# Products of a zeroed tile in front of TensorE's waits in a four-layer encoder step

## The chip, the cores and the metric

The kernel runs on one core of a Trainium2 chip. The metric is the device time of one execution in microseconds (us). The engines are TensorE (PE; its weight loads are shown apart as PEld), VectorE (DVE), ScalarE (ACT), GpSimd (POOL) and SyncE (SP), which issues most DMAs. Each engine works through its own instructions in the order of the program, and they meet at semaphores: `wait_ge` holds an engine until a count is reached, `then_inc` raises it when an instruction ends.

## The reference

One inference step of a trunk of four layers on 320 rows of width 1024 (64 rows of a running stream, 256 of a new one). Each layer is RMSNorm, a token mixer, a residual add, RMSNorm, a gated feed-forward block with a causal convolution of width 3, and a residual add. The mixers are, in order: sparse attention with an indexer (layer 0), an RWKV-7 state mixer (layer 1), multi-head latent attention (layer 2), sparse attention again (layer 3).

```python
hn = _rmsnorm(x, w['n_mix'][i])
# layers 0, 3: q, k, v, qi, ki, wi = split(h @ w_in); top keys by the indexer; softmax; @ w_out
# layer 1:
xx = h_prev - h
xm = h[:, :, None, :] + xx[:, :, None, :] * mu
r, k, v = xr @ w_rkv[0], xk @ w_rkv[1], xv @ w_rkv[2]
w_log = -softplus(-(w0 + tanh(xw @ w1) @ w2)) - 0.5
a = sigmoid(a0 + (xa @ a1) @ a2);  g = sigmoid(xg @ g1) @ g2
kk = normalise(k * k_k);  k = k * (1 + (a - 1) * k_a)
y, S = _wkv7_scan(S0, r, decay, k, v, -kk, kk * a)
y = groupnorm(y) + sum(r * k * r_k) * v
out = (y * g) @ w_out
x = x + out
x = x + (silu(gate) * val) @ w_down      # gate, val: convolution of rmsnorm(x) @ w_up
```

The outputs are the rows of y, the new keys, values and latents, and the states.

## The kernel before, in words

Activations lie transposed: 128 partitions of the width, 320 rows in the free dimension, eight such tiles for the width 1024. All dense weights stream through two slots as numbered slabs: SP loads a slab into `raw`, ACT copies it to `hi` (rounded to fp32r, L1749), DVE or POOL subtracts to `lo` (L2294, L681). `product` (L960 to L972) multiplies a slab's 128 columns with an activation tile in three fp32r products per contraction step: hi by XH (L968), hi by XL (L969), lo by XH (L970). Small products are plain fp32 calls.

There is no scheduler: the order of the work is the order in which each engine's program is written, and `ready(n)` or a `wait_ge` marks what TensorE needs next. The places that matter here, all in TensorE's program:

- `dsa` (L1169), layers 0 and 3. In layer 0 slab 0 comes in two halves: TensorE waits for `first_lo` (L1190) and runs the first halves of tiles 0 and 1, then the second ones. `project(t)` does tiles 2 to 6. After tile 2 comes `mean_square` (L984), the sum of squares of the first norm: ACT squares the x tiles, POOL adds them up in `ssq` (L670). After tile 5 `weights_turn` (L1196) waits for `wi_scaled` (DVE L2466, WIf) and turns three tiles (L980). Then tile 6, and the indexer's products `dots` (L1232 to L1238), for which POOL writes the last rotated key (L893). Index scores (ACT relu, DVE), top keys and the attention follow.
- `ffn` (L1085). At the end of layer 0's block TensorE runs `mean_square` for layer 1's norm (`norm_next(layer) not in LATE` holds for layer 0 alone). The last residual tile goes DVE, ACT square, POOL sum before it. Behind it: ACT root, DVE reciprocal `rstd`, DVE HN (L2537).
- `pe_rwkv` (L1308), layer 1: 24 low-rank calls (`low_rank`, L1314) on HN, XX and K as DVE makes them; then 24 tiles of K, R and V (i = 0 to 23, two to a slab, eight to each of the three), the first of each eight with a wait for every contraction step (`mix_done`: ACT XH, DVE XL L2564). Between the tiles stand `lora_rows` (L1342), `key_sums` (L1350), `key_fans` (L1357, which waits for DVE's AR, L2612) and `bonus_sums` (L1363, which waits for DVE's xn, L2626). POOL works on the keys (L756 to L763). Then the chunked recurrence (L1403 and around), and at its end the output products (`out_part`, L1617), the last of which wait for YH (DVE L2711).

Of the kernel before, what the change touches and what calls it, by code (L numbers as in the profile page):

```python
# [158 lines left out]
def build(nc, i_, o_):  # L159
# [61 lines left out]
    with ExitStack() as ctx:  # L221
# [16 lines left out]
        def sem(name):  # L238
            return ctx.enter_context(nc.semaphore(name))
# [22 lines left out]
        rstd = sb("rstd", [128, T])  # L262
        xn = sb("xn", [128, 2, T])
        uout = sb("uout", [128, 2, 128])
        over = base[0]
        limit = nc.sbuf_usable_end

# [212 lines left out]
        (state_in, rec_begun, rec_pe, rec_act, rec_dve, kb_done, p0_done, iqt_done, y_sq, y_var, y_root, y_normed, y_parts) = map(  # L480
            sem, "state_in rec_begun rec_pe rec_act rec_dve kb_done p0_done iqt_done y_sq y_var y_root y_normed y_parts".split())
        state_stored, gate_done, u_copied = sem("state_stored"), sem("gate_done"), sem("u_copied")
        md_done, yh_parts = sem("md_done"), sem("yh_parts")
        row_ms, row_rms, row_scale, y_scaled, y_sample_scaled, y_tail_scaled, y_stored = map(
            sem, "row_ms row_rms row_scale y_scaled y_sample_scaled y_tail_scaled y_stored".split())
        cqn_done, lat_parts, kc_rope, latf_done, head_roped = map(sem, "cqn_done lat_parts kc_rope latf_done head_roped".split())
# [160 lines left out]
        def _(pool):  # L647
            chain = Chain(pool, pool_c)
            stores = [0]

            def store(dst, src):
                pool.dma_start(dst, src).then_inc(stored, 16)
# [296 lines left out]
        def _(pe):  # L949
            ident, ones = C("ident"), C("ones")  # L950

            def ready(n):

                pe.wait_ge(w_lo, n + 1)

            def parts(n):
                s = slabs[n]
                return (t[n % 2][:, 0:s.kt * s.w].rearrange("p (k w) -> p k w", w=s.w) for t in (hi, lo))
# [126 lines left out]
            def ffn(layer):  # L1085
                F0 = NF * layer
                u0, d0 = first_slab[layer, "up"], first_slab[layer, "down"]
                jn = norm_of[layer, "ffn"]

                def up(f, n, j, first, before=None):  # L1090
                    pe.wait_ge(w_lo, f + (u0 + 1))
                    if not first:
                        pe.wait_ge(u_raw, f + (F0 - 1))
                    for h in range(2):
                        product(psum[2 * j + h][:, 0:T], n, 128 * h, lambda k: XH[:, k, :], lambda k: XL[:, k, :],
                                before=before if h == 0 else None)
                        if before and h == 0:
                            mean_square(jn)

                for j in range(2):  # L1100
                    up(j, u0 + j, j, True, x_ready(jn) if j == 0 else None)
                with pe.Fori(1, NF // 2) as i:
                    for j in range(2):
                        up(i * 2 + j, u0 + j, j, False)

                xb = 8 * xs_of[norm_next(layer)]

                def down_half(n_ready, n, j, half, before=None):
                    pe.wait_ge(w_lo, n_ready)
                    product(psum[4 + j][:, 0:T], n, 0, lambda k: GH[:, 11 * half + k, :],  # L1110
                            lambda k: GL[:, 11 * half + k, :], start=(half == 0), stop=(half == 1), before=before)

                last = norm_next(layer) == norm_final

                def rows_turn(m):

                    pe.wait_ge(xn_done, XN[norm_final] + m + 1)
                    if m >= 2:
                        pe.wait_ge(y_copied, m - 1)
                    for z, (c, n_) in enumerate(TILES):  # L1120
                        b = psum[3] if m == KD - 1 and z == 2 else psum[m % 2]
                        ins = turn(b[0:n_, 128 * z:128 * z + 128], XG[:, m % 2, c:c + n_])
                    ins.then_inc(y_turned, 1)

                def down(m, j):
                    for half in range(2):
                        if half == 0:
                            pe.wait_ge(x_done, m + (xb - 1))
                        down_half(m * 2 + (d0 + half + 1), d0 + 2 * j + half, j, half)
                        if half == 0 and last:  # L1130
                            rows_turn(m - 1)

                def row_sums():

                    spans = [slice(0, 128), slice(64, 192), slice(192, 320)]
                    pe.wait_ge(ssq_done, norm_base[norm_final] + 7)
                    for z, c in enumerate(spans):
                        pe.matmul(psum[7][:, z:z + 1], ssq[:, c], ones[:, 0:1], start=(z == 0), stop=False, skip_group_check=True)
                    pe.wait_ge(sq_done, norm_base[norm_final] + 8)
                    for z, c in enumerate(spans):  # L1140
                        ins = pe.matmul(psum[7][:, z:z + 1], sq[:, (norm_base[norm_final] + 7) % 2, c], ones[:, 0:1], start=False, stop=True,
                                        skip_group_check=True)
                    ins.then_inc(row_ms, 1)

                pe.wait_ge(g_done, F0 + 11)
                down_half(d0 + 1, d0, 0, 0)
                down_half(d0 + 2, d0 + 1, 1, 0)
                pe.wait_ge(g_done, F0 + 21)
                down_half(d0 + 3, d0 + 2, 0, 1, lambda k: k == 10 and pe.wait_ge(g_done, F0 + 22))

                pe.wait_ge(ust_done, F0 + NF)
                for z in range(2):
                    ins = turn(psum[6][0:88, 128 * z:128 * z + 128], ust[:, z, :, :].rearrange("p r c -> p (r c)"))
                ins.then_inc(ust_turned, 1)
                down_half(d0 + 4, d0 + 3, 1, 1)
                if last:
                    rows_turn(0)
                    for m in range(2, KD):
                        down(m, m % 2)
                    rows_turn(KD - 1)  # L1160
                    row_sums()
                else:
                    with pe.Fori(1, KD // 2) as i:
                        for j in range(2):
                            down(i * 2 + j, j)
                    if norm_next(layer) not in LATE:
                        mean_square(norm_next(layer))

            def dsa(layer):  # L1169
# [17 lines left out]
                            first=0 if low else 4, end=4 if low else None)  # L1187

                if layer == 0:
                    pe.wait_ge(first_lo, 1)  # L1190
                    first_halves(0, True, x_ready(jn))
                    first_halves(1, True)
                    ready(s0)
                    first_halves(0, False, x_ready(jn))
                    first_halves(1, False)
                def weights_turn():  # L1196
                    pe.wait_ge(wi_scaled, inst + 1)
                    for z, (c, n_) in enumerate(TILES):
                        last = turn(psum[6][0:n_, 128 * z:128 * z + 128], WIf[:, c:c + n_])
                    last.then_inc(wi_turned, 1)  # L1200
# [107 lines left out]
            def pe_rwkv(layer):  # L1308
# [7 lines left out]
                        ins.then_inc(lora_mid, 1)  # L1316

                narrow, wide = slice(0, 128), slice(128, 256)
                for z in range(2):
                    tiles = range(4 * z, 4 * z + 4)  # L1320
                    for k in tiles:
                        pe.wait_ge(lora_mix, 9 * z + k % 4 + 1)
                        low_rank(4, L1, narrow, HN, k, opens=k == 0)
                    pe.wait_ge(lora_mix, 9 * z + 5)
                    for k in tiles:
                        low_rank(4, L1X, narrow, XX, k, closes=k == KD - 1)
                    for k in tiles:
                        pe.wait_ge(lora_mix, 9 * z + 6 + k % 4)
                        low_rank(6, L1, wide, K, k, opens=k == 0, closes=k == KD - 1)
# [37 lines left out]
                bonus_at = {18: (0,), 19: (1,), 20: (2,), 22: (3, 4), 23: (5, 6, 7)}  # L1367
                for i in range(24):
                    n, j = s0 + i // 2, i // 8
                    ready(n)  # L1370
                    if i >= 2:
                        pe.wait_ge(rkv_evac, i - 1)
                    xh, xl = ((XH, XL), (XH2, XL2), (XH, XL))[j]
                    product(psum[i % 2][:, 0:T], n, 128 * (i % 2), lambda k: xh[:, k, :], lambda k: xl[:, k, :],
                            before=(lambda k: pe.wait_ge(mix_done, KD * j + k + 1)) if i % 8 == 0 else None)
                    if i < 4:
                        lora_rows(2 * i)
                        lora_rows(2 * i + 1)
                    for m in sums_at.get(i, ()):
                        key_sums(m)  # L1380
                    for m in fans_at.get(i, ()):
                        key_fans(m)
                    for m in bonus_at.get(i, ()):
                        bonus_sums(m)

                HALF = (slice(0, 64), slice(64, 128))
# [244 lines left out]
                    out_part(m, YL, wh, before)  # L1631
                rows_turn(c)
                state_turn(c)
                pe.wait_ge(yh_parts, CHUNKS)
                for m in range(2):
                    out_part(m, YH, wh, last_)
# [1281 lines left out]
```

## Time and profile before

| | us |
|---|---|
| median of 3 runs | 1670.91 |
| lowest, highest | 1668.04, 1674.12 |
| the profiled execution | 1669.34 |
| its span, first to last instruction | 1667.5 |
| mean granted TensorE clock | 0.991 of full |
| TensorE, DVE, ACT, POOL busy | 96%, 68%, 50%, 43% |

The profile is of one execution. Its page gives busy time by engine, the span in 40 slices, the DMA queues, the chain of work that ended last, and the costliest groups of instructions. Its trace was asked for the instructions of stretches in order of time, for waits, and for windows with the granted clock of TensorE. In a row "x8" means that eight records of a kind are merged; a plain fp32 call leaves two records, an fp32r call or a transpose one. The end of a TensorE record is modelled, so the distance between starts is the better measure of what one costs.

### The profile page before, as it was taken

To read this page: it belongs to the slowest core of one execution; us is meant where nothing else is said; L and a number is where in the kernel's file an instruction comes from. 1 tells how busy PE (TensorE), PEld (TensorE's weight loads), DVE (VectorE), ACT (ScalarE), POOL (GpSimd) and SP (SyncE) were. 2 spreads that over 40 slices of the span, in tenths; PEclk is the share of its full clock that TensorE was granted. 3 is DMA by queue.
4 is the path that set the end of the run, shared out by engine and by line. 5 is a ranking of instruction groups with operands and counts; after the bars stand their busy time and mean duration, and the time that the engine had idled before them with its cause. 6 is when DMAs were issued, how large, how long until landed. Compare 5 with 4: busy or idle time off the path is not lost.

```text
span 1667.5 us, 36145 instructions
## 1 busy us (share of the span) xinstructions
PE 1594.7 (96%) x13605; PEld 1518.7 (91%) x13605; DVE 1130.1 (68%) x1978; ACT 840.2 (50%) x1589; POOL 713.4 (43%) x702
## 2 busy tenths in 40 slices
PE   6989999998989998999999998999999999999998
PEld 6869999996778998999999877999999878999997
DVE  4877777636478566777764766877764787777743
ACT  4465655534653433455543475555543455655633
POOL 6654666210046211366621450466621764566500
PEclk9999999998999999999999999999999999999999
DMA  7224556453231003555545421455545512555453
GB/s 234 92 69 130 151 151 167 124 156 99 89 102 33 10 4 98 152 146 147 141 138 170 145 83 52 136 147 147 142 138 165 162 53 84 156 147 147 132 147 106
DMA packets 331754, 203.94 MB, mean 122 GB/s; under 512 B 7752, under 2 KB 327384, under 8 KB 331520
## 3 DMA queue, kind: packets, MB, share of 16 engines
q1 hardware_dynamic: 329136, 195.45, 40.6%
q0 software_dynamic: 1776, 5.60, 1.1%
q8 instruction: 74, 1.21, 0.3%
q10 hardware_dynamic: 736, 1.41, 0.2%
q14 instruction: 32, 0.26, 0.1%
HBM read 198.95 MB, written 3.39 MB: 121 GB/s over the span
## 4 chain that ended last, share of the span: by engine, by line
PE 79%; DVE 8%; ACT 5%; POOL 4%; issue 4%; DMA 0%; SPq 0%; DVEq 0%; POOLq 0%; ACTq 0%
PE bank L968 22%; PE bank L970 22%; PE bank L969 22%; PE bank L1403 4%; DVE lo L2294 2%; ACT hi L1749 2%; POOL lo L681 1%; PE bank L980 1%; PE bank L1314 1%; POOL ssq L670 1%; POOL qsin L701 1%; PE bank L1617 1%; PE bank L1022 1%; PE bank L1342 1%; DVE xn L2547 0%
## 5 line engine op out<-in xcount | busy, mean ns | idle before, releaser
L968 PE MATMUL bank<-XH,hi 128*128 128x320 f32 (+1 forms) x1912 | 602.8, 315 | 15.7 <-DVE lo L2324 8.8
L2294 DVE TENSOR_TENSOR lo<-raw,hi 128x2048 fp32r<-128x2048 f32 (+2 forms) x195 | 413.3, 2120 | 283.7 <-ACT hi L1749 283.7
L969 PE MATMUL bank<-XL,hi 128*128 128x320 f32 (+1 forms) x1912 | 594.1, 311 | 0.0
L970 PE MATMUL bank<-XH,lo 128*128 128x320 f32 (+1 forms) x1912 | 594.0, 311 | 0.0
L1749 ACT ACTIVATE hi<-raw 128x2048 fp32r<-128x2048 f32 (+2 forms) x203 | 356.0, 1754 | 72.3 <-PE bank L970 67.2
L968 PEld LDWEIGHTS bank<-XH,hi 128*128 128x128 f32 (+1 forms) x1912 | 361.8, 189 | 27.7 <-DVE lo L2324 8.8
L969 PEld LDWEIGHTS bank<-XL,hi 128*128 128x128 f32 (+1 forms) x1912 | 362.0, 189 | 1.3
L970 PEld LDWEIGHTS bank<-XH,lo 128*128 128x128 f32 (+1 forms) x1912 | 361.8, 189 | 0.0
L730 POOL TENSOR_TENSOR upad<-upad,rpad 128x656 f32<-128x656 f32 x88 | 146.7, 1667 | 204.6 <-ACT upad L1857 204.6
L734 POOL COPY ust<-upad 128x4 f32 (+1 forms) x176 | 215.2, 1253 | 13.5 <-POOL upad L730 13.0
L968 PE MATMUL bank<-GH,hi 128*128 128x320 f32 x704 | 218.6, 311 | 1.8 <-DVE lo L2294 1.8
L970 PE MATMUL bank<-GH,lo 128*128 128x320 f32 x704 | 217.5, 309 | 0.0
L969 PE MATMUL bank<-GL,hi 128*128 128x320 f32 x704 | 217.5, 309 | 0.0
L670 POOL TENSOR_TENSOR ssq<-ssq,sq 128x320 f32<-128x320 f32 x66 | 75.2, 1139 | 281.0 <-ACT sq L1905 221.0
L1856 ACT COPY upad<-bank 128x320 f32<-128x320 f32 x176 | 72.4, 437 | 243.5 <-PE bank L970 243.5
L2411 DVE SCALAR_TENSOR_TENSOR conv<-upad,V,conv 128x320 f32<-128x320 f32 x352 | 170.2, 545 | 0.0
L968 PEld LDWEIGHTS bank<-GH,hi 128*128 128x128 f32 x704 | 132.2, 188 | 2.5 <-DVE lo L2294 2.5
L969 PEld LDWEIGHTS bank<-GL,hi 128*128 128x128 f32 x704 | 132.2, 188 | 0.0
L970 PEld LDWEIGHTS bank<-GH,lo 128*128 128x128 f32 x704 | 132.2, 188 | 0.0
L1867 ACT ACTIVATE conv<-upad,V 128x320 f32<-128x320 f32 x176 | 106.7, 666 | 4.1 <-POOL upad L730 4.1
L1905 ACT ACTIVATE sq<-xT 128x320 f32<-128x320 f32 (+1 forms) x32 | 15.1, 472 | 129.1 <-DVE xT L2434 129.1
L968 PE MATMUL bank<-OH,hi 128*128 128x320 f32 x174 | 55.2, 317 | 2.6 <-DVE lo L2294 1.4
(390 smaller groups left out, 2240.3 us busy)
## 6 DMA issues: line engine op xcount, KB each, us to landing
raw<-in_f_w_up SPq DMA_DIRECT2D x176, 512.0 KB, 5.0
raw<-in_f_w_down SPq DMA_DIRECT2D x64, 704.0 KB, 4.7
raw<-in_a_w_in SPq DMA_DIRECT2D x13, 1024.0 KB, 5.5
raw<-in_b_w_rkv SPq DMA_DIRECT2D x12, 1024.0 KB, 5.2
raw<-in_a_w_out SPq DMA_DIRECT2D x8, 1024.0 KB, 5.2
raw<-in_b_w_out SPq DMA_DIRECT2D x4, 1024.0 KB, 5.3
raw<-in_c_w_out SPq DMA_DIRECT2D x4, 1024.0 KB, 5.1
raw<-in_c_w_uq SPq DMA_DIRECT2D x3, 1024.0 KB, 5.1
```

The costliest lines, as they stand in the source:

```text
L670: pool.tensor_tensor(ssq[:, :], ssq[:, :], sq[:, (c - 1) % 2, :], ALU.add).then_inc(ssq_done, 1)
L730: pool.tensor_tensor(upad[:, j, :, 2:2 + n_], upad[:, j, :, 2:2 + n_], rpad[:, 2:2 + n_].rearrange("p (o n) -> p o n", o=1).to_broadcast([ ...
L734: ins = pool.tensor_copy(ust[:, seg, :, :].rearrange("p r (h f) -> p h r f", h=2)[:, :, :, bass.ds(f, 1)].rearrange("p h r f -> p h (r f)" ...
L968: pe.matmul(out, a, xh(k), start=(start and k == 0), stop=False)
L969: pe.matmul(out, a, xl(k), start=False, stop=False)
L970: last = pe.matmul(out, b, xh(k), start=False, stop=(stop and k == kt - 1))
L1403: last = pe.matmul(out[r_, col(q)], lhs(e, r_, q), rhs(e, r_, q), start=opens and (closes or q == 0), stop=closes, skip_group_check=True)
L1749: act.activation(hi[n % 2][:, 0:w_], raw[n % 2][:, 0:w_], ACT.Copy).then_inc(w_hi, 1)
L1856: act.copy(segs(upad[:, j, h, :], 2), rows_of(ps[h][:, 0:T]))
L1867: ins = act.activation(rows_of(conv[:, j, h, :]), segs(upad[:, j, h, :], 2), ACT.Identity, scale=V[:, bass.ds(f + (w_ + NF * h), 1)], bias ...
L2294: dve.tensor_tensor(lo[n % 2][:, 0:w_], raw[n % 2][:, 0:w_], hi[n % 2][:, 0:w_].bitcast(F32), ALU.subtract).then_inc(w_lo, 1)
L2411: dve.scalar_tensor_tensor(out=rows_of(conv[:, j, h, :]), in0=segs(upad[:, j, h, :], tap), scalar=V[:, bass.ds(f + (w_ + NF * h), 1)], in1 ...
```

## The change

A tile `still` (128x128, fp32) is added in SBUF and set to zero by POOL at the head of its program. `keep(count, b)` issues `count` fp32 products of `still` by `still` into the first 128 columns of PSUM bank b; nobody reads them. TensorE gets them ahead of its waits: 46 in three blocks before layer 0's first product, 50 in `weights_turn` of layer 0, 17 before the `mean_square` between layers 0 and 1, 28 before layer 1's low-rank calls, 10 and seven times 3 before the contraction steps of tile i = 0, 14 before tile i = 10, 4, 2 and 13 before key fans 2, 4 and 7, 6 and 14 before bonus sums 4 and 7, and 9 before the last output products of layer 1: 234 calls in all. Nothing is removed or moved.

```diff
--- before.py
+++ after.py
@@ -262,6 +262,7 @@
         rstd = sb("rstd", [128, T])
         xn = sb("xn", [128, 2, T])
         uout = sb("uout", [128, 2, 128])
+        still = sb("still", [128, 128])
         over = base[0]
         limit = nc.sbuf_usable_end
 
@@ -480,7 +481,7 @@
         (state_in, rec_begun, rec_pe, rec_act, rec_dve, kb_done, p0_done, iqt_done, y_sq, y_var, y_root, y_normed, y_parts) = map(
             sem, "state_in rec_begun rec_pe rec_act rec_dve kb_done p0_done iqt_done y_sq y_var y_root y_normed y_parts".split())
         state_stored, gate_done, u_copied = sem("state_stored"), sem("gate_done"), sem("u_copied")
-        md_done, yh_parts = sem("md_done"), sem("yh_parts")
+        md_done, yh_parts, still_set = sem("md_done"), sem("yh_parts"), sem("still_set")
         row_ms, row_rms, row_scale, y_scaled, y_sample_scaled, y_tail_scaled, y_stored = map(
             sem, "row_ms row_rms row_scale y_scaled y_sample_scaled y_tail_scaled y_stored".split())
         cqn_done, lat_parts, kc_rope, latf_done, head_roped = map(sem, "cqn_done lat_parts kc_rope latf_done head_roped".split())
@@ -647,6 +648,7 @@
         def _(pool):
             chain = Chain(pool, pool_c)
             stores = [0]
+            pool.memset(still[:, :], 0.0).then_inc(still_set, 1)
 
             def store(dst, src):
                 pool.dma_start(dst, src).then_inc(stored, 16)
@@ -953,6 +955,11 @@
 
                 pe.wait_ge(w_lo, n + 1)
 
+            def keep(count, b):
+
+                for _ in range(count):
+                    pe.matmul(psum[b][:, 0:128], still[:, :], still[:, :], start=True, stop=True)
+
             def parts(n):
                 s = slabs[n]
                 return (t[n % 2][:, 0:s.kt * s.w].rearrange("p (k w) -> p k w", w=s.w) for t in (hi, lo))
@@ -1164,6 +1171,7 @@
                         for j in range(2):
                             down(i * 2 + j, j)
                     if norm_next(layer) not in LATE:
+                        keep(17, 3)
                         mean_square(norm_next(layer))
 
             def dsa(layer):
@@ -1187,6 +1195,12 @@
                             first=0 if low else 4, end=4 if low else None)
 
                 if layer == 0:
+                    pe.wait_ge(still_set, 1)
+                    keep(24, 0)
+                    pe.wait_ge(xh_done, 2)
+                    keep(14, 0)
+                    pe.wait_ge(first_hi, 1)
+                    keep(8, 0)
                     pe.wait_ge(first_lo, 1)
                     first_halves(0, True, x_ready(jn))
                     first_halves(1, True)
@@ -1194,6 +1208,8 @@
                     first_halves(0, False, x_ready(jn))
                     first_halves(1, False)
                 def weights_turn():
+                    if layer == 0:
+                        keep(50, 6)
                     pe.wait_ge(wi_scaled, inst + 1)
                     for z, (c, n_) in enumerate(TILES):
                         last = turn(psum[6][0:n_, 128 * z:128 * z + 128], WIf[:, c:c + n_])
@@ -1316,6 +1332,7 @@
                         ins.then_inc(lora_mid, 1)
 
                 narrow, wide = slice(0, 128), slice(128, 256)
+                keep(28, 3)
                 for z in range(2):
                     tiles = range(4 * z, 4 * z + 4)
                     for k in tiles:
@@ -1367,20 +1384,31 @@
                 bonus_at = {18: (0,), 19: (1,), 20: (2,), 22: (3, 4), 23: (5, 6, 7)}
                 for i in range(24):
                     n, j = s0 + i // 2, i // 8
+                    if i == 10:
+                        keep(14, 6)
                     ready(n)
                     if i >= 2:
                         pe.wait_ge(rkv_evac, i - 1)
                     xh, xl = ((XH, XL), (XH2, XL2), (XH, XL))[j]
+
+                    def mixed(k):
+                        if i == 0:
+                            keep(3 if k else 10, 7)
+                        pe.wait_ge(mix_done, KD * j + k + 1)
+
                     product(psum[i % 2][:, 0:T], n, 128 * (i % 2), lambda k: xh[:, k, :], lambda k: xl[:, k, :],
-                            before=(lambda k: pe.wait_ge(mix_done, KD * j + k + 1)) if i % 8 == 0 else None)
+                            before=mixed if i % 8 == 0 else None)
                     if i < 4:
                         lora_rows(2 * i)
                         lora_rows(2 * i + 1)
                     for m in sums_at.get(i, ()):
                         key_sums(m)
                     for m in fans_at.get(i, ()):
+                        keep({2: 4, 4: 2, 7: 13}.get(m, 0), 6)
                         key_fans(m)
                     for m in bonus_at.get(i, ()):
+                        if m in (4, 7):
+                            keep(14 if m == 7 else 6, 2)
                         bonus_sums(m)
 
                 HALF = (slice(0, 64), slice(64, 128))
@@ -1631,6 +1659,7 @@
                     out_part(m, YL, wh, before)
                 rows_turn(c)
                 state_turn(c)
+                keep(9, (PE_AT["y", c] - 1) % 8)
                 pe.wait_ge(yh_parts, CHUNKS)
                 for m in range(2):
                     out_part(m, YH, wh, last_)
```

## Rows read from the trace of the kernel before

**Rows 1.** the page: busy time, and the chain that ended last, by engine

```profile
PE 1594.7 (96%) x13605; PEld 1518.7 (91%) x13605; DVE 1130.1 (68%) x1978; ACT 840.2 (50%) x1589; POOL 713.4 (43%) x702
...
PE 79%; DVE 8%; ACT 5%; POOL 4%; issue 4%; DMA 0%; SPq 0%; DVEq 0%; POOLq 0%; ACTq 0%
```

**Rows 2.** windows: busy PE, PEld, DVE, ACT, POOL; granted clock; DMA share, GB/s

```profile
40.00:50.00 10.00, 9.38 (x49) 8.23 (x50) 5.16 (x6) 5.50 (x10) 9.39 (x10) 0.75 0.34 103
...
390.00:400.00 10.00, 10.00 (x33) 6.83 (x32) 9.79 (x21) 0.00 (x0) 0.00 (x0) 0.84 0.23 74
...
410.00:420.00 10.00, 9.85 (x47) 7.56 (x49) 3.74 (x5) 3.88 (x11) 1.01 (x2) 0.83 0.34 107
...
480.00:490.00 10.00, 7.91 (x37) 5.32 (x38) 5.36 (x8) 7.06 (x9) 9.37 (x9) 0.94 0.39 124
490.00:500.00 10.00, 10.00 (x52) 10.00 (x53) 6.07 (x7) 3.26 (x6) 7.88 (x9) 0.72 0.25 88
```

**Rows 3.** TensorE in order of time, 8 to 47 us: start, duration, instruction

```profile
8.80 0.64 PE L968 MATMUL bank<-XH,hi 128*128 128x320 f32 x1 [8.80 <-DVE lo L2324]
...
14.29 0.31 PE L970 MATMUL bank<-XH,lo 128*128 128x320 f32 x1
...
21.76 0.31 PE L970 MATMUL bank<-XH,lo 128*128 128x320 f32 x1
23.12 0.78 PE L984 MATMUL bank<-ssq,con 128*128 128x320 f32 x2 [1.05 <-POOL ssq L670]
...
40.49 0.85 PE L980 MATMUL bank<-con,WIf 128*64 128x128 f32 x3 [6.03 <-DVE WIf L2466]
...
46.68 0.54 PE L1232 MATMUL bank<-KIT,QIT 64*64 64x192 f32 x2
```

**Rows 4.** waits of TensorE, 380 to 430 us: waited for, total, times, longest

```profile
PE bank L1314 <- DVE HN L2537: 3.5, 1, 3.5
PE bank L968 <- DVE XL L2564: 2.4, 5, 1.2
PE bank L984 <- POOL ssq L670: 2.0, 1, 2.0
```

**Rows 5.** waits of TensorE, 430 to 700 us

```profile
PE bank L1363 <- DVE xn L2626: 2.6, 2, 1.9
PE bank L1357 <- DVE AR L2612: 2.4, 3, 1.7
PE bank L968 <- DVE lo L2294: 2.3, 2, 1.7
...
PE bank L968 <- ACT AR L2051: 0.5, 1, 0.5
```

**Rows 6.** TensorE in layer 2's attention: fp32 calls on 96x128 weights

```profile
1002.33 0.61 PE L992 MATMUL bank<-KC,QT 96*128 96x128 f32 x4
1002.78 1.03 PE L994 MATMUL bank<-KC,QT 96*128 96x256 f32 x4
```

**Rows 7.** TensorE, layer 1's low-rank calls and first tile

```profile
389.41 4.23 PE L1314 MATMUL bank<-HN,L 128*128 128x320 f32 x8 [3.48 <-DVE HN L2537]
393.48 2.32 PE L1314 MATMUL bank<-XX,L1X 128*128 128x320 f32 x8
395.63 2.32 PE L1314 MATMUL bank<-K,L 128*128 128x320 f32 x8
...
404.27 0.39 PE L968 MATMUL bank<-XH,hi 128*128 128x320 f32 x1
...
413.04 1.07 PE L1342 MATMUL bank<-LT,L 64*128 64x320 f32 x4
```

**Rows 8.** TensorE, transposes in layer 2

```profile
1004.21 1.09 PE L980 MATMUL bank<-con,LS3m 128*128 128x128 f32 x8
```

**Rows 9.** TensorE, last output products of layer 1

```profile
658.29 1.97 PE L1617 MATMUL bank<-YH,hi 128*128 128x64 f32 x16 [1.05 <-DVE YH L2711]
```

**Rows 10.** POOL in order of time, its first work after the constants

```profile
9.43 0.71 POOL L657 DMA_DIRECT2D con<-in_const  x1 [8.98 <-DMA xT<-in_x]
```

## The prediction

> **What bounds the kernel now.** I read the page first: TensorE is busy for 96% of the span and the chain that ended last is 79% TensorE, with the rest spread over four engines [rows 1]. So nearly everything that TensorE does later ends the kernel later, outside a few stretches in which it waits. The windows say where its clock fell: the granted clock averages 0.75, 0.84, 0.83, 0.94 and 0.72 of full in five stretches of 10 us, which at the two levels 2.4 and 1.2 GHz is 5.0, 3.2, 3.4, 1.2 and 5.6 us at the lower one [rows 2]. Each follows or holds a wait. Third, the waits themselves. In front of most of them the change puts its products: 8.8 us before the first product, 1.05 for ssq (untouched), 6.03 for the scaled index weights WIf [rows 3]; 2.0 for ssq, 3.5 for HN, 2.4 in five pieces for XL (the first 1.2) [rows 4]; then in layer 1's mixer 2.3 in two pieces for a weight's low half (1.7 and 0.6), 2.4 in three for AR from the fans (1.7 the longest, so 0.7 in the others), 2.6 in two for xn (1.9 and 0.7) [rows 5], and 1.05 for YH at its end [rows 9]. Last, the spacing of the kernel's first products, since the clock column has no record of a change there: product 0 starts at 8.80, product 20 at 14.29 and product 71 at 21.76, so it is 0.274 us until 14.29 and 0.1465 after it. The first is the lower clock, and costs 5.49 - 20 x 0.1465 = 2.56 us [rows 3].
>
> **What one added product costs.** All turns on this. keep(n, b) issues n products of fp32 128x128 by 128 columns. They need no data, but TensorE's queue is in order: what stands behind them waits until the last is through, however early its data comes. No row has this very shape. The nearest is the fp32 product of 128 columns on 96x128 weights: two calls (one per head) leave four records, which take from 1002.33 to 1002.78, so 0.1125 us a record and **0.225 us a call** [rows 6]. The long shape agrees: eight records of 320 columns are four calls and take 393.48 to 395.63, 0.269 a record, 0.54 a call; 128/320 of that is 0.215 [rows 7]. I take 0.225, the nearest shape. Upper end: eight transposes with 128-wide fp32 loads take 1.09 us, 0.136 a record; if such a load sets the pace, a call is 0.27 [rows 8]. Lower end: sixteen one-record products of only 64 columns take 1.97 us, 0.12 each; a call that behaved as one such record would cost 0.12 [rows 9]. The Trainium skill ("TensorE: Matmul & The Clock Gate", "Back-to-back issue gap") gives about 81 ns per product at 128 columns in a stream of load and product pairs. By it the 50 products would take 4.1 us instead of 11.3, every block would fit in its wait and the sum would be that of the first rival; the fp32 rows of this kernel are almost three times as long, and I go by them.
>
> So 0.225 x n against the wait that each block fills: 50 give 11.25 us against 6.0; 17 give 3.8 against 2.0; 28 give 6.3 against 3.5; 14 give 3.15 against 1.7; 13 give 2.9 against 1.7; 14 give 3.15 against 1.9; 6 give 1.35 against 0.7; 9 give 2.0 against 1.0. Each block is nearly twice as long as its wait, and the excess lands on TensorE's own queue.
>
> **Part 1, the head of layer 0.** The memset on POOL is one small instruction; POOL does nothing before its DMA at 9.43, which waits 8.98 us for x, so it costs nothing; without that cover it would be of the order of POOL's ordinary copies, under 1 us [rows 10]. The waits on still_set, xh_done and first_hi are all met before first_lo, which the next instruction waits for anyway. TensorE can begin at about 0.8 us, after the memset. 46 calls are 10.35 us at the full clock; in this stretch the clock took 5.5 us of work to rise, so the calls until then cost double, about 2.5 us more. The first real product comes at 0.8 + 10.35 + 2.5 = 13.7 instead of 8.80, but at the full clock; 72 products of 0.1465 end at 24.2, where before ssq let the sum of squares start at 23.12 [rows 3]. TensorE is 1.1 us late there. Had the blocks been short, the 2.56 us won would have run into this same wait for ssq: **nothing is won here in either case**.
> Then TensorE comes to weights_turn 1.1 late, at 35.6 (before: 40.49 less the wait of 6.03, 34.46). 50 calls end at 46.8, three transposes add 0.3, tile 6 with 24 products 3.6: 50.8. Before, the first dots product stood at 46.68 [rows 3]. So +4.1 us, though the 5.0 us at the lower clock (2.3 us lost) are gone; that is counted, since tile 6 is at full speed. Behind dots are ACT's relu, DVE's scores, POOL's rope and the attention, all fed by it, so I let all of it pass. The clock gain alone would be worth little: the gap before the dots is only some tenths and waits on POOL's last rope sum.
>
> **Part 2, into layer 1.** keep(17) ends 3.8 - 2.0 = 1.8 after ssq is ready; the sum of squares, root, reciprocal and HN follow 1.8 later. TensorE itself issues 28 calls, 6.3 us, against 3.5: the low-rank products start 1.8 + 2.8 = 4.6 after 389.41, at 394.0. Their 48 records took 14.84 us before, partly at the lower clock, and take 48 x 0.269 = 12.9 now: 1.9 back, so 2.7 late at the end [rows 7]. The next tile took 413.04 - 404.27 = 8.8 us, eight steps of three products with waits between them [rows 4, 7]. Now: 10 calls 2.25, first step 0.44, then seven steps of 0.44 + 3 x 0.225 = 1.115 (the waits of about 0.3 vanish in that), 7.8; together 10.5, so +1.7. 0.4 of lower clock on the low-rank rows behind it comes back. Part 2: 2.7 + 1.7 - 0.4 = **+4.0**.
>
> **Part 3, the rest of layer 1's mixer.** keep(14) before slab 5 is 1.4 over its wait, but short waits follow (0.5 for ACT's AR, 0.6 for the next low half, and the 0.7 of the shorter fan waits), so about 0.3 is left; with keep(4) and keep(2), 0.9 and 0.45 against 0.5 and 0.3, it is 0.6 at the last fan. keep(13) adds 1.2: 1.8 late there. The lower clock that began in this wait is gone: 1.2 and 5.6 us of it in the last two windows, worth 3.4 [rows 2, 5]. Net -1.6. What is late next is POOL with the keys, 9.4 and 7.9 us busy in these two windows; I take -1.3 for what passes. keep(6) is 0.65 over; keep(14) is 1.25 over and stands behind the 0.65: **+1.9** before the state products. keep(9) is 1.0 over [rows 9]: **+1.0**.
>
> **Sum:** 4.1 + 4.0 - 1.3 + 1.9 + 1.0 = +9.7 us. The profiled execution took 1669.34 us for a span of 1667.5; it comes to 1679.0. It lies 1.57 under the median of the three runs, 1670.91, so on the median I forecast **1680.6**, 0.58% slower.
>
> **Rivals.**
> *Short products (0.14).* A call costs 0.12 [rows 9]. It decides below about 0.13, where all blocks fit. Then only clock is won: 0 in layer 0 (ssq and POOL cover it), 1.9 in the low-rank products, 0.6 in the tile behind them, and of 3.4 about 2.0 before POOL's keys bind: -4.5, so **1666.4**, faster by just under 0.3%; single terms could carry it over. For it: no row has the call's very shape. Against: [rows 6, 7]. The Trainium skill's 81 ns would give the same time.
> *Absorbed in layer 0 (0.14).* The dots come 4.1 late but POOL, ACT and DVE set the attention (TensorE has waits there as well). If they do not inherit the delay the sum is 5.6 and the time **1676.5**; with half of part 2 absorbed too, 1674. Against: their inputs come from the same late tiles.
> *Load-paced products (0.10).* A call is 0.27 [rows 8]. 0.045 more for each: 46 and 50 calls add 2.1 and 2.3, 76 in part 2 3.4, the last 42 of part 3 1.9: 9.7 more, **1690.3**.
> *The zeros do not hold the clock (0.02).* The full clock falls as before or blocks run at half speed: the gains of 1.9 and 3.4 go and calls double in part, **about 1697**.
> My forecast has 0.60, its own range 1675 to 1686 from half-passed parts and 0.215 to 0.24 a call.
>
> **How the numbers follow.** The range 1671 to 1690 takes in the forecast, the absorbed case and nearly the load-paced one; it leaves out the short products, the last rival and thin tails, 0.2 in all. About 0.3%, 5.0 us, is what a measurement of this kernel can tell from no change. Faster than 1665.9: 0.08, from the short products. Within: 0.16, the rest of them, the low half of the absorbed case and a tail. Slower than 1675.9: 0.76.
>
> **What would show each step.** TensorE's count should rise from 13605 by 468 (234 calls, two records each) and the new line's records should follow each other at 0.11 us, 0.22 a call. First real product near 13.7; WIf transposes near 47; dots near 51; low-rank products near 398 (389.41 + 4.1 + 4.6); no window of layers 0 and 1 below full clock after the first microseconds. In the waits, WIf, HN and xn should vanish, replaced by no wait at all. I am wrong if the records stand at 0.06 us, if the dots stay near 46.7, or if the clock falls again behind the blocks.

## The result, and the profile after

| | before | after |
|---|---|---|
| median of 22 runs each, us | 1671.86 | 1677.93 |
| lowest, highest | 1666.19, 1678.29 | 1675.26, 1682.24 |
| profiled execution, its span | 1669.34, 1667.5 | 1678.3, 1676.5 |
| mean granted clock, profiled; mean of many runs | 0.991; 0.988 (the 87 runs of the three sets below) | 0.997; 0.997 (these 22) |

The ratio is 1.0038, 95% interval 1.0028 to 1.0048: **6.1 us slower**, over the 0.3% that a measurement can tell. Direction and range of the forecast (+9.7 us) held; its size on the median did not. Between the two profiled executions the step is +9.0 us. One run of the entry alone (2614.56 us at a granted clock of 0.556) and one of entry and late (2253.95 us at 0.654) were slow executions of another kind and stand in none of the figures below.

The page of the kernel after, the lines that answer to [rows 1], and its row of the new line's weight loads (busy time, mean ns):

```profile
PE 1636.4 (98%) x14073; PEld 1566.2 (93%) x14073; DVE 1128.9 (67%) x1978; ACT 840.1 (50%) x1589; POOL 714.4 (43%) x703
...
PE 86%; DVE 5%; ACT 3%; issue 3%; POOL 2%; DVEq 0%; ACTq 0%; POOLq 0%
...
L961 PEld LDWEIGHTS bank<-still 128*128 128x128 f32 x468 | 57.2, 200 | 2.6 <-issue 1.1
```

TensorE has 468 records more, two for each of 234 calls. Its share of the chain rose from 79 to 86% and took over what DVE, ACT and POOL had: waits became work that nobody reads.

TensorE of the kernel after in order of time (start, duration, instruction; the first two blocks, then what answers to [rows 3]):

```profile
1.00 13.37 PE L961 MATMUL bank<-still 128*128 128x128 f32 x92 [1.00 <-POOL still L651]
14.12 0.39 PE L975 MATMUL bank<-XH,hi 128*128 128x320 f32 x1
...
24.77 0.46 PE L991 MATMUL bank<-ssq,con 128*128 128x320 f32 x1
...
35.89 11.32 PE L961 MATMUL bank<-still 128*128 128x128 f32 x100
47.05 0.49 PE L987 MATMUL bank<-con,WIf 128*64 128x128 f32 x3
50.98 0.54 PE L1248 MATMUL bank<-KIT,QIT 64*64 64x192 f32 x2
```

The 50 calls before WIf take 47.05 - 35.89 = 11.16 us, 0.223 each, where the wait had been 6.03. The kernel's own first product stands at 14.12 (before 8.80), the dots at 50.98 (46.68): +4.3. No row from 14 to 50 us has a wait in brackets any more.

The same view at the entry to layer 1 (answers to [rows 4, 7]):

```profile
387.27 3.96 PE L961 MATMUL bank<-still 128*128 128x128 f32 x34
391.06 0.70 PE L991 MATMUL bank<-ssq,con 128*128 128x320 f32 x2
391.60 6.41 PE L961 MATMUL bank<-still 128*128 128x128 f32 x56
397.85 2.32 PE L1330 MATMUL bank<-HN,L 128*128 128x320 f32 x8
...
410.88 2.40 PE L961 MATMUL bank<-still 128*128 128x128 f32 x20
413.03 0.39 PE L975 MATMUL bank<-XH,hi 128*128 128x320 f32 x1
413.56 0.83 PE L961 MATMUL bank<-still 128*128 128x128 f32 x6
414.14 0.39 PE L975 MATMUL bank<-XH,hi 128*128 128x320 f32 x1
...
421.40 0.81 PE L1359 MATMUL bank<-LT,L 64*128 64x320 f32 x4
```

The blocks stand end to end with the real work. The low-rank calls start at 397.85, 8.44 later than before; the full clock gives 1.9 back (they take 12.92 us, not 14.84); one contraction step and its three added calls take 1.11 us; what follows the tile starts at 421.40 against 413.04, +8.36.

The waits of TensorE after, 440 to 720 us (waited for, total, times, longest; from 380 to 440 there are none):

```profile
PE bank L1431 <- issue: 2.2, 4, 0.9
PE bank L1553 <- issue: 1.8, 1, 1.8
...
PE bank L975 <- DVE lo L2323: 0.2, 1, 0.2
```

xn and AR are gone from the list, the low half is down from 2.3 to 0.2, and WIf, ssq and HN are gone ahead of it. The windows over the same stretches as [rows 2], and then four of 1 us behind the state mixer (columns as there):

```profile
40.00:50.00 10.00, 10.00 (x86) 10.00 (x85) 2.33 (x4) 2.53 (x5) 6.88 (x8) 1.00 0.26 81
390.00:400.00 10.00, 10.00 (x77) 9.22 (x77) 7.50 (x12) 3.61 (x3) 0.45 (x1) 1.00 0.66 210
410.00:420.00 10.00, 10.00 (x81) 9.66 (x80) 8.19 (x15) 4.93 (x11) 1.02 (x2) 1.00 0.01 2
480.00:490.00 10.00, 10.00 (x67) 8.71 (x65) 9.11 (x11) 7.39 (x6) 1.42 (x2) 1.00 0.43 136
490.00:500.00 10.00, 9.98 (x65) 8.29 (x65) 4.98 (x7) 5.35 (x7) 9.77 (x10) 1.00 0.50 161
```

```profile
669.00:670.00 1.00, 1.00 (x6) 1.00 (x6) 0.83 (x1) 0.00 (x0) 0.00 (x0) 0.57 0.91 266
670.00:671.00 1.00, 1.00 (x5) 1.00 (x5) 0.00 (x0) 0.00 (x0) 0.00 (x0) 0.50 1.07 345
671.00:672.00 1.00, 1.00 (x6) 1.00 (x5) 0.14 (x1) 0.00 (x0) 0.00 (x0) 0.50 1.09 384
672.00:673.00 1.00, 1.00 (x7) 1.00 (x6) 0.93 (x3) 0.47 (x1) 0.09 (x1) 0.72 1.08 351
```

In the five stretches where it had been 0.72 to 0.94, the clock is full: the change does what it says. But it fell once more where it had not before, at 669.1, with TensorE busy all the time.

### The profile page after: what moved, and what is told of

It reads as the page before. It is cut to its first block, busy times and chain, and to the rows that moved or that the text cites. A ratio compares the mean times of both kernels' runs of the same rounds, so it can differ in the third digit from the quotient of the medians.

```text
span 1676.5 us, 37081 instructions
## 1 busy us (share of the span) xinstructions
PE 1636.4 (98%) x14073; PEld 1566.2 (93%) x14073; DVE 1128.9 (67%) x1978; ACT 840.1 (50%) x1589; POOL 714.4 (43%) x703
## 4 chain that ended last, share of the span: by engine, by line
PE 86%; DVE 5%; ACT 3%; issue 3%; POOL 2%; DVEq 0%; ACTq 0%; POOLq 0%
PE bank L975 23%; PE bank L977 23%; PE bank L976 23%; PE bank L1431 4%; PE bank L961 3%; DVE lo L2323 2%; ACT hi L1778 2%; POOL lo L683 1%; PE bank L987 1%; PE bank L1330 1%; PE bank L1645 1%; PE bank L1029 1%; PE bank L1359 1%; POOL qsin L703 1%; PE bank L1001 0%
## 5 line engine op out<-in xcount | busy, mean ns | idle before, releaser
L975 PEld LDWEIGHTS bank<-XH,hi 128*128 128x128 f32 (+1 forms) x1912 | 358.7, 188 | 11.3 <-issue 6.9
L961 PEld LDWEIGHTS bank<-still 128*128 128x128 f32 x468 | 57.2, 200 | 2.6 <-issue 1.1
```

The source lines that it names most:

```text
L961: pe.matmul(psum[b][:, 0:128], still[:, :], still[:, :], start=True, stop=True)
L975: pe.matmul(out, a, xh(k), start=(start and k == 0), stop=False)
```

## The experiments

All in five rounds, in three sets; each set has its own runs of the kernel before (medians 1671.74, 1673.63 and 1672.12 us of 29, 35 and 23 runs). The counts of the diffs are those of keep.

**Half the calls (first set).** If a call is 0.223 us, a wait of w us is filled by w / 0.223 calls; the counts are cut to that.

```diff
-keep(24, 0) ... keep(14, 0) ... keep(8, 0) ... keep(50, 6)
+keep(10, 0) ... keep(5, 0) ... keep(3, 0) ... keep(26, 6)
-keep(17, 3) ... keep(28, 3) ... keep(3 if k else 10, 7)
+keep(8, 3) ... keep(15, 3) ... keep(1 if k else 5, 7)
-keep(14, 6) ... {2: 4, 4: 2, 7: 13} ... keep(14 if m == 7 else 6, 2) ... keep(9, ...)
+keep(7, 6) ... {2: 2, 4: 1, 7: 7} ... keep(8 if m == 7 else 3, 2) ... keep(4, ...)
```

> All blocks stay, each cut to fit its wait at 0.223 us a call: 10, 5, 3 at the start, 26, 8, 15, 5 and seven times 1, 7, then 2, 1, 7, then 3, 8, and 4. Theory (length): the loss of the changed kernel is what the blocks overrun their waits by, and the clock they hold is worth about 4.5 us; so 4 to 7 us faster than before, dots back near 46.7 us, low-rank products near 389.5, end of their block 2 us earlier than before. Rival (presence): the calls cost something beside their length (issue, PSUM, the queue), then it stays level with before or slower, and a call lasts longer than 0.225. Rival (hold): shorter blocks leave gaps in which the clock falls again; then level with before, with windows below full clock at the same places.

1667.20 us, ratio 0.9974 (0.9960 to 0.9988): faster than before by 4.3 us by the ratio, and 10.7 below the change as made. Dots at 45.60, 1.1 ahead of the kernel before. TensorE in order of time, and POOL's last operation on the key that the dots need:

```profile
35.86 5.96 PE L961 MATMUL bank<-still 128*128 128x128 f32 x52
41.66 0.49 PE L987 MATMUL bank<-con,WIf 128*64 128x128 f32 x3
45.60 0.54 PE L1248 MATMUL bank<-KIT,QIT 64*64 64x192 f32 x2
```

```profile
43.88 0.87 POOL L895 TENSOR_TENSOR KIT<-qcos,qsin 64x320 f32<-64x320 f32 x1
```

That operation took 2.80 us in the trace of the kernel before, so its key was ready at 46.6 and not at 44.8. The 1.1 us at the dots rest on this.

The 4.3 us are at the low end of the expected 4 to 7. The idea is sound and the counts were not: the excess over the waits is what makes the change slower.

**The same without the head of layer 0 (first set).** The counts above, the four blocks in layer 0's head at zero.

> e1 without the blocks of layer 0's head (10, 5, 3 and 26 gone; those from 8 before the sum of squares on stay). Theory: nothing is won in the head, since ssq and POOL's rope end behind TensorE in either case; so the time of e1 within 1 us, dots near 46.7 us with TensorE idle 6 us before the weights' transposes. Rival (head pays): the head's clock, 2.6 and 2.3 us, counts; then 2 to 5 us slower than e1.

1665.99 us, ratio 0.9971 (0.9955 to 0.9986), the lowest of all, but not to be told from the 1667.20 with the head's blocks: their means differ by 0.6 us with a standard error of 0.8. So no gain from the head's blocks can be seen even when they fit, as the prediction had it from the wait for ssq behind them. In this trace the dots wait for POOL's key until 46.61. Windows of this kernel at the entry, 0.84 and 0.83 before:

```profile
390.00:400.00 10.00, 9.23 (x35) 6.27 (x34) 9.79 (x21) 0.00 (x0) 0.00 (x0) 1.00 0.23 77
410.00:420.00 10.00, 9.94 (x56) 6.82 (x54) 2.87 (x3) 5.25 (x11) 1.01 (x2) 1.00 0.31 106
```

**Calls of half the length (first set).** The prediction's rival of short products, made real: the tile rounded to fp32r, so that a call leaves one record; all counts as in the change.

```diff
-still = sb("still", [128, 128])
+still = sb("still", [128, 128], F32R)
```

> The changed kernel with its 234 calls, but the zeroed tile is fp32r, so a call is one record instead of two. Theory (length): a call takes about 0.11 to 0.12 us, blocks fit their waits, dots near 46.7 us; 3 to 6 us faster than before if the clock holds. Rival (hold): one-record calls stream 128 columns in 0.11 us, about half of what the array can take, and the clock falls in or after the long blocks; then within 2 us of before. Rival (presence): as slow as the changed kernel, +6 us, since the number of calls is the same.

1669.88 us, ratio 0.9986 (0.9971 to 1.0002): no difference that can be told from the kernel before, and 8.1 below the change. By the ratio that is 2.3 us faster where 3 to 6 were expected, nearer to the rival that the clock would fall. TensorE in order of time, POOL's last operation on the key, and windows behind the first dots:

```profile
34.25 5.70 PE L961 MATMUL bank<-still 128*128 128x128 f32 x50
40.51 0.52 PE L987 MATMUL bank<-con,WIf 128*64 128x128 f32 x3 [0.57 <-DVE WIf L2495]
46.72 0.54 PE L1248 MATMUL bank<-KIT,QIT 64*64 64x192 f32 x2 [2.17 <-POOL KIT L895]
```

```profile
43.88 2.79 POOL L895 TENSOR_TENSOR KIT<-qcos,qsin 64x320 f32<-64x320 f32 x1
```

```profile
46.00:48.00 2.00, 1.28 (x8) 0.94 (x10) 2.00 (x3) 0.83 (x1) 2.00 (x3) 0.86 0.46 40
48.00:50.00 2.00, 2.00 (x8) 0.86 (x5) 1.89 (x1) 0.47 (x2) 2.00 (x1) 0.50 1.01 357
```

A call is 0.114 us; the 50 fit their wait, and WIf is waited for by 0.57 only. TensorE is then early at the dots and waits 2.17 us there for POOL's key instead (before, some tenths): the dots do not move (46.72 against 46.68), and behind that wait the clock falls. What is filled ahead is waited for, and lost, at the next producer, if that one is late: here the operation on the key took 2.79 us, with half the calls 0.87. What sets its length is open.

**Eight moving columns (first set).** The records stay, 468 of them, and most of the columns go.

```diff
-pe.matmul(psum[b][:, 0:128], still[:, :], still[:, :], start=True, stop=True)
+pe.matmul(psum[b][:, 0:8], still[:, :], still[:, 0:8], start=True, stop=True)
```

> The changed kernel with the same 234 fp32 calls, each with 8 moving columns in place of 128. If the weight load sets the pace of a call, it lasts as long (0.22 us) and TensorE is as busy; if the columns do, it is much shorter. Theory (length, clock by streamed columns): where the block is as long as before the clock falls as in the kernel before or lower, and the time is 4 to 12 us above the changed kernel when the load paces, and about level with the kernel before (within 3 us) when the columns pace. Rival (clock by busy instructions): the clock holds all the same; then the changed kernel's time if the load paces, or 3 to 6 us under the kernel before if the columns do.

1715.92 us, ratio 1.0265 (1.0238 to 1.0292): 38 us above the changed kernel, where 4 to 12 were expected. Its first block, its windows in the block before WIf, and the kernel after's in the same block:

```profile
1.00 19.79 PE L961 MATMUL bank<-still 128*128 128x8 f32 x92 [1.00 <-POOL still L651]
```

```profile
44.60:49.00 4.40, 4.40 (x43) 4.40 (x41) 0.50 (x4) 0.44 (x1) 4.32 (x6) 1.00 1.00 394
50.00:60.00 10.00, 10.00 (x49) 10.00 (x48) 0.63 (x1) 0.00 (x0) 5.43 (x7) 0.50 0.10 30
```

```profile
37.00:45.00 8.00, 8.00 (x74) 8.00 (x73) 2.08 (x4) 0.88 (x2) 7.76 (x10) 1.00 0.68 244
```

The first block takes 19.6 us where it took 13.1 with 128 columns. At the two paces below, 0.102 and 0.204 a record, that is the lower clock for almost all of it; the clock column has no record of it. Two things follow.

First, at full clock a record takes 4.40 / 43 = 0.102 us with 8 columns and 8.00 / 74 = 0.108 with 128: the columns are nearly free. A fixed price of each record is not what is left, since in the kernel before fp32 records with 64-wide weights and 64 moving columns follow each other at 0.96 / 32 = 0.030 us:

```profile
649.12 1.15 PE L1525 MATMUL bank<-UV,JJ 128*64 128x64 f32 x32 [0.16 <-PE bank L1403]
650.08 1.13 PE L1509 MATMUL bank<-UV,KBt 128*64 128x64 f32 x32
```

So it is the load of 128-wide weights that sets the pace.

Second, with 8 columns the clock falls to its lower level inside the block, while the busy column shows 10.00 of 10.00; there a record takes 10.00 / 49 = 0.204. So calls with few columns are as dear and did not hold the clock.

**Each part alone (second set).** All three have the change's own counts: the 96 calls of layer 0's head; the 76 at the entry to layer 1 (17, 28, 10 and seven times 3); the 62 of its later waits.

> The changed kernel with the blocks of layer 0's head alone (24, 14, 8 and 50), the other 138 calls gone. Theory (length): first product near 14, weights' transposes near 47, dots near 51, so 4.3 us behind the profiled kernel before; low-rank products near 393.7. In the medians somewhat less, since the kernel before also loses the clock here in every run: +2 to +4.5 us. Rival (absorbed): later waits of the attention swallow the delay, so the last product of layer 0 is under 2 us late and the time within 1.5 us of before.

> The changed kernel with the blocks between layers 0 and 1 alone (17, 28, 10 and seven times 3). Theory (length): 1.6 us late at the sum of squares, 4.1 at the low-rank products, 2.2 at their end, 4.1 at the low-rank rows; the clock holds from the sum of squares to there. On the medians +1 to +4 us, as the kernel before pays more for its clock here in most runs than in the profiled one. Rival: nothing of the clock is run-dependent here; then +4 to +5 us.

> The changed kernel with the later blocks of layer 1's mixer alone (14; 4, 2, 13; 6, 14; 9). From the two traces: +0.4 at the fans, +1.3 at the last one, -1.7 at the first bonus sum, +1.1 at the last, +0.9 at the output products; so between -1.5 and +2 us. The three parts (e5, e6, e7) should add to the changed kernel's +6 within 3 us if they are independent; a sum well over it says that one block pays for another's clock.

Head 1674.64 us, ratio 1.0006 (0.9993 to 1.0020), +1.0 us by the ratio. Entry 1673.72, 0.9999 (0.9983 to 1.0015), -0.2. Late 1670.26, 0.9985 (0.9972 to 0.9997), -2.5. All three lie below what was expected of them (+2 to +4.5, +1 to +4, -1.5 to +2). For the head the number is the one of the rival, absorbed, but the trace is not: its down products of layer 0 start at 307.08, 4.1 late. In the traces the delays stand where they should: dots at 50.74 with the head's blocks, low-rank calls at 393.45 with the entry's (389.41 + 4.04). But the three sum to -1.7 us, where the whole gave +6.3 by its ratio: the parts do not add.

**The entry with half its calls (second set).** 8, 15, 5 and seven times 1, nothing else.

> The fitted blocks between layers 0 and 1 alone (8, 15, 5 and seven times 1). Theory: most of what e4 wins (5.7 us) comes from here, where the clock is at the lower level for over 6 us in the profiled kernel before: 2.5 to 4 us faster than before, the rest with the fans. Rival: the win of e4 is mostly the fans'; then under 1.5 us.

1669.59 us, ratio 0.9978 (0.9965 to 0.9991): -3.7, against -0.2 with the change's counts. Low-rank calls at 389.27, where they were, at full clock. The counts alone decide between a gain and none. This one came as expected (2.5 to 4 us faster).

**The whole again beside its pairs (third set).** To see whether the missing 8 us are the set of runs or lie in the parts together.

> The changed kernel, unaltered, measured beside the pairs of its parts. Open is why its three parts measured alone (head +1.0, entry -0.2, late part -2.5 us) sum to -1.7 while the whole gave +6.3. Theory A, the clock can be won back only once: each part alone cut lost clock in the typical run by 5 to 8 us, which sums to some 18, but all parts together cut it by 15 and the delays add in full. Then the whole stands again at +5 to +8 us. Rival B, the set of runs: the parts were timed on another set of runs of the kernel before, with a median 1.9 us higher, and the whole would come to +2 or less beside that one; then the parts add.

> The 96 calls in layer 0's head and the 76 at the entry to layer 1, nothing later. In the trace the two delays are both on TensorE's own queue and must add: dots near 51, low-rank products near 397.5, rows of the first tile near 421. In time: if the parts simply add, +1.0 - 0.2 = +0.8 us. By theory A, part of the missing 8 us belongs to this pair, the one with most products: +3 to +5.

> The head's 96 calls and the 62 of layer 1's later waits, none at the entry. If the parts add: +1.0 - 2.5 = -1.5 us. By theory A: between 0 and +3. Here the low lies with the entry, untouched: the granted clock should fall there (HN's wait) as before, with low-rank products at 389.4 + 4.2 = 393.6.

> The 76 calls at the entry to layer 1 and the 62 later ones, nothing in layer 0. If the parts add: -0.2 - 2.5 = -2.7 us. By theory A: between -1 and +2. Dots near 46.6, low-rank products near 393.4.

Whole 1678.46 us, ratio 1.0039 (1.0026 to 1.0052): +6.5 by the ratio, as at first, so rival B, the set of runs, falls. Head and entry 1679.45, 1.0048 (1.0034 to 1.0062), +8.0. Head and late 1674.72, 1.0020 (1.0010 to 1.0029), +3.3. Entry and late 1675.15, 1.0016 (1.0004 to 1.0027), +2.7. Each pair is above the sum of its parts, as theory A has it, and above the range it gave as well, the first by 3.0 us, the others by 0.3 and 0.7. In the traces the pairs' positions are near those expected (dots 50.68 and low-rank calls 397.50 for head and entry, 392.70 for head and late), but for entry and late, whose low-rank calls are at 395.05 for 393.4: 1.6 of that arose in layer 0, where nothing was changed. Both kernels wait for 1.83 us before 112.2 or 112.3 us there; from 110 to 116 us the granted clock was 0.72 in this execution and 1.00 in the profiled one of before. So the same wait costs the clock in one execution and not in another. For the entry left alone behind the head, the window:

```profile
390.00:400.00 10.00, 7.29 (x19) 4.93 (x20) 9.83 (x17) 2.87 (x2) 0.00 (x0) 0.66 0.53 177
```

The clock falls at HN's wait as before, to 0.66 here.

Every run has its granted clock beside its time, so each mean can be split. A run's time times (1 - clock) is its lost clock; the rest is the time less that. Means over the runs, in us, against the kernel before of the same set (whose lost clock is 19.7, 21.2 and 21.0 and whose rest is 1651.7, 1651.8 and 1651.3):

| kernel | time | lost clock | rest |
|---|---|---|---|
| head | +1.9 | -4.6 | +6.4 |
| entry | +0.3 | -7.6 | +7.9 |
| late | -2.1 | -7.7 | +5.5 |
| sum of the three | 0.0 | **-19.9** | **+19.9** |
| the whole | +6.1 | **-14.9** | **+21.0** |
| head, entry | +6.6 | -11.3 | +17.9 |
| head, late | +2.6 | -9.3 | +11.9 |
| entry, late | +2.4 | -11.3 | +13.6 |
| half the calls | -4.3 | -11.2 | +7.0 |
| half, without head | -4.9 | -10.1 | +5.3 |
| half, entry alone | -3.1 | -7.1 | +4.0 |
| fp32r calls | -1.7 | -10.5 | +8.8 |
| 8 columns | +44.4 | +18.0 | +26.3 |

The times of one kernel have a standard deviation of 1.4 to 2.7 us in its 5 to 12 runs, so a difference here is good to about 1 us, and the sum of three to about 2. The rest adds (19.9 against 21.0): delays on one in-order queue sum up. The lost clock does not (19.9 against 14.9), and the gap of 5.0 is about twice its standard error of 2.4. The kernel before loses 21 us, and in its trace 2.3 of the 15 lie behind TensorE's last instruction, where no block could win them; so about 18 were there to win, and the parts cannot each have won their own 19.9. The whole still loses 6, in its first trace 3.7 behind TensorE's last instruction and 1.7 at 669. That is theory A's account. Counted at one us for each us of lost clock it carries 5.0 of the 6.1 us between the sum and the whole; at the 0.73 found below it carries 3.7. So it is supported, not shown. Open are the rest of the 6.1 us, the pair of head and entry, whose rest is 3.5 above its two parts' (5 runs), and which clock falls of a typical run are the shared ones. The traces can't tell: there is one of each kernel (two of the whole), and at 655 to 675 us the clock fell in that of the head alone but in neither that of before nor that of the late part.

## Why the prediction came out as it did

**What a call costs: right in size, not in its reason.** 0.225 was taken from [rows 6]; the blocks show 0.223. The short and the load-paced rival fall with it in price (0.12 and 0.27). But the 8-column run shows that the pace is the load's after all, at 0.10 to 0.11 a record, not the transposes' 0.136 of [rows 8]. The Trainium skill's 81 ns per product at 128 columns ("TensorE: Matmul & The Clock Gate", "Back-to-back issue gap") does not hold for these fp32 calls: a record takes 0.108 and a call two of them.

**Part 1: right.** Forecast first product 13.7, sum of squares 24.2, dots 50.8; found 14.12, 24.77, 50.98, and a delay of 4.3 for 4.1. The first block took 13.12 us, 2.9 over its 46 calls at full clock, for 2.5. All of it passed: the down products of layer 0 start at 307.31 for 302.99, 4.3 late too, so the rival "absorbed in layer 0" falls in the trace.

**Part 2: right.** Forecast +4.0; found 8.36 - 4.30 = +4.06, with a step of 1.11 us for 1.115.

**Part 3: right by its signs, with one term too large.** Up to the first bonus sums -1.6 was found for -1.3 (513.28 against 506.51, +6.77 from +8.36). The two bonus blocks were put at +1.9; the first state products are at +7.88 from +6.77, so +1.1: of the smaller block's 0.65 some 0.4 passed on, of the larger one's 1.25 some 0.7. The block before the last output products costs +0.9 for +1.0.

**Not foreseen, from 640 us on.** At 643 us the profiled execution of before has a stall of 2.4 us put down to issue; that of after lacks it and has one of 1.78 at 656. Then comes the clock fall at 669.1, +1.5 us. From the first state products (531.87) to the first output tile of three products a step on YH (L968, 664.31) it is 132.4 us in the trace of before and 133.5 after; in four kernels with nothing added in that stretch (head, entry, half entry, head and entry) it is 135.5, 131.7, 135.0 and 133.2. So single executions scatter by more here than the two traces differ. "No window below full clock" was right up to 669 us.

**The step that failed: the median.** The sum for the profiled execution was 1679.0; it took 1678.3. The prediction then set the same +9.7 on the median. That takes the clock that one execution lost as what every run loses. The three sets hold 87 runs of the kernel before; their mean by granted clock, six of the nine levels:

```
clock  0.984   0.986   0.988   0.990   0.991   0.992
runs       4      16      11      12       7       2
us    1677.6  1674.4  1671.9  1669.9  1668.0  1666.4
```

Through all 87 a us of lost clock goes with 0.73 us of time. The profiled execution, at 0.991, lost 1669.34 x 0.009 = 15.0 us; the mean run, at 0.9877, loses 20.6. So a typical run had 5.6 us more of it, 5.6 x 0.73 = 4.1 us of time; the profiled one was also 1.3 slow for its clock (1669.34 against 1668.0). 9.0 - 4.1 + 1.3 = 6.2, and the medians give 6.1. The prediction knew that the profiled execution lay under the median of three, by 1.57, and carried this over to the kernel after, where the profiled one (1678.3) is level with the median (1677.93). So the step was 3.6 us too large; that the median of before came out at 1671.86 and not 1670.91 hid 0.9 of it. After the change the clock hardly varies (0.995 to 0.999), so its profile stands for its median. That lost clock and time go together over the runs is measured; that each single loss costs 0.73 of itself is not.

**The chances.** The forecast's mechanism was the one that happened in the trace, the slower side was right, and the size lies at the low end of its own range of 1675 to 1686.

## What to carry to other kernels

Filler work in front of a wait is paid for in full past the wait's end, and the queue does not forgive it: count it from the measured price of one call (here 0.22 us for an fp32 128x128 call, 0.11 in fp32r) and stay at or under the wait, since with half the calls the same places turned +6.3 us into -4.3. Put it only where nothing else is waited for right behind; in layer 0's head the next producer (ssq, then in the fp32r run POOL's key) took the gain away, and leaving the blocks out cost nothing (-4.8 us by its ratio). And before a gain from the clock is summed, look at the granted clock of many runs, not at that of the one execution that has a trace.

## What the hardware showed that was not expected

- A record of 8 moving columns takes 0.102 us and one of 128 columns 0.108, both on fp32 128x128 weights at the full clock; at the lower one the 8-column record takes 0.204. At 320 columns the product does show: 0.269 [rows 7].
- A busy TensorE did not hold the clock by that alone. The block of 8-column calls before WIf ran at 100% busy and the granted clock went to 0.50, all through 50 to 60 us. The Trainium skill ("TensorE: Matmul & The Clock Gate", "Part 1: The HAM clock gate") has the gate watch how busy the array has been; the records' busy time is not that measure here. The fall at 669.1 after the change stands behind output products of 64 columns, again with TensorE busy throughout; the kernel before ran the same products from 658 to 662 us and kept the full clock behind them, so their part in it is open.
- Products of zeros with 128 columns hold the full clock: from 37 to 45 us TensorE ran nothing else, at 1.00.
- One POOL operation on 64x320, the last on layer 0's key, took 0.85 to 0.87 us in seven of the fourteen traces and 2.79 or 2.80 in the other seven, on the same operands.
- The kernel before, unchanged, spreads over 12 us within one set of runs (1666.2 to 1678.0 in the first), and the granted clock, between 0.984 and 0.992 in all three sets, goes with it.
